# Mixture panels loaded in one 2 MB transfer each, into three double homes of the ring

## The chip, the cores and the metric

The kernel runs on one core of one Trainium2 chip. The metric is the time of one execution on the device, in microseconds (us), as the median of several runs. Five engines of the core work side by side and meet only at semaphores: TensorE (PE, with its weight loads as PEld), VectorE (DVE), ScalarE (ACT), GpSimd (POOL) and SyncE (SP). SP issues most transfers, POOL the others; all of them are carried out by the core's 16 DMA engines. "PEq" or "SPq" is the instruction queue (the sequencer) of an engine.

## The reference

Two transformer blocks in float32 over 256 tokens of width 1024. The first has a short-convolution and pooling mixer, cross attention, a dense feed-forward stage, a convolution module, cross attention again and a mixture of 8 experts. The second has a hybrid mixer (two attentions and a recurrence), attention to a memory, and a mixture of 16 experts in 4 groups. The change touches the two mixtures alone:

```python
def moe_swiglu(xn, router, w_gu, w_down):           # first: 8 experts, hidden width 3584
    ...
    for e in range(N_EXPERTS):
        out = out + comb[..., e:e + 1] * swiglu(xn, w_gu[e], w_down[e])

def swiglu(xn, w_gu, w_down):
    g, u = jnp.split(xn @ w_gu, 2, axis=-1)
    return (jax.nn.silu(g) * u) @ w_down

def _grouped_moe(x, router_w, router_b, w1, w3, w2):  # second: 16 experts, hidden width 512
    ...
    for e in range(N_EXPERTS_2):
        hid = jax.nn.silu(xt @ w1[e]) * (xt @ w3[e])
        out = out + gate_dense[:, e, None].astype(xt.dtype) * (hid @ w2[e])
```

Each token uses two experts. The weights of the first mixture are 8 x (1024 x 7168 + 3584 x 1024) floats, those of the second 16 x 3 x 1024 x 512; every one of them is read from memory once.

## The kernel before

The kernel is written directly in semaphores: for each engine there is one function (`@block.sync`, `@block.tensor`, ...) whose instructions run in the order of the text, and every meeting of two engines is a counter that one raises and the other waits for. No scheduler moves anything.

**Panels and halves.** A weight matrix comes in panels of 512 columns (gate, up) or 512 rows (down), 2 MB each. In the mixtures a panel is handled as two halves of 1 MB, [128 partitions x 2048 floats]. `stream(c)` (lines 168 to 175) lists the halves of one group of experts in the order in which they are used: gate 0, up 0, then for each further chunk gate, up, and the down panel of the chunk before, and the last down panel; each panel gives two halves that follow one another. In the first mixture a group is one expert with 7 chunks, so N = 42 halves, and 8 groups; in the second a group is 4 experts with one chunk each, so N = 24 halves, and 4 groups (`MOES`, lines 162 to 165). Together that is 8 x 42 + 4 x 24 = 432 halves.

**The ring.** `ring` (line 212) has 7 homes of one half. Half j of a group goes to home j % slots, with slots = 7 in the first mixture and 6 in the second. Outside of the mixtures the same memory is used as three homes of a whole panel (`SLOTS = 3`, `load`, lines 456 to 467), and home 6 for other things.

**The path of a half.** SP waits until the home is free and issues the transfer (lines 476 to 481). ACT waits for its landing and writes the rounded copy `w_high` (lines 1481 to 1483). DVE subtracts it from the ring's copy and writes the remainder `w_low` (lines 2055 to 2057); that raises `split`, which is both what PE waits for (line 970) and what frees the home for SP (line 479). PE then makes 12 matmuls of 512 columns with the half: four products of three matmuls each (`product`, lines 697 to 703). `w_high` and `w_low` have three places each (`SPLITS = 3`), so ACT may start on half j only when PE is done with half j - 3 (`read`, line 1482).

**What else runs in the loop.** Per chunk: ACT's silu (line 1462), DVE's gated product (line 2033), four transposes on PE (`turn_hidden`, line 965), and their split by ACT (line 1466) and DVE (line 2037). Once per group: ACT copies the last group's outputs (line 1447, before half 3), and POOL then adds them to the sums in memory with an indirect transfer of 512 KB (line 572); DVE picks the next group's tokens (line 1971, before half 8), PE finds their places (line 925), and POOL loads the rows with another indirect transfer (line 576); PE turns them before half N - 4 (line 932).

**Where the order comes from.** SP's queue holds the transfers in the order of the halves, each behind its own wait for `split`. Each home has a semaphore of its own, `landed0` and so on, raised by 16 for each transfer. The home of half j is freed by the split of half j - slots.

Of the kernel before, what the change touches and what calls it, by code (L numbers as in the profile page):

```python
# [21 lines left out]
P = 128  # L22
# [4 lines left out]
PANEL = 512  # L27
# [126 lines left out]
for _j in range(2):  # L154
# [5 lines left out]


MOES = {
    1: dict(groups=8, members=1, chunks=7, slots=7, experts=8),
    2: dict(groups=4, members=4, chunks=1, slots=6, experts=16),
}

# [32 lines left out]
def program(nc, ins, const_in, out):  # L199
    ctx = ExitStack()  # L200
    with ctx:
# [252 lines left out]
        @block.sync  # L454
        def _(sync):
            def load(i, wait):
                pieces, sem, value = panels[i]
                if wait:

                    sync.wait_ge(S(panels[i - SLOTS][1]), panels[i - SLOTS][2])  # L460
                for where, src in pieces:
                    n = src.shape[2]
                    if where == "rows":
                        dst = slot_rows(slot(i))[:, 0:src.shape[1], :]
                    else:
                        dst = slot_kn(slot(i))[:, :, where[0]:where[0] + n]
                    sync.dma_start(dst, src).then_inc(S(f"landed{slot(i)}"), 16)

            def experts(k, source):
                c = MOES[k]  # L470
                slots, halves = c["slots"], stream(c)

                sync.sem_inc(moe_sem(k, "split"), slots)

                def group(g, turn):
                    for j, (kind, chunk, half) in enumerate(halves):

                        sync.wait_ge(moe_sem(k, "split"), turn * len(halves) + (j + 1))
                        src = source(kind, g, chunk, half)
                        dst = ring[:, j % slots, :].rearrange("p (k n) -> p k n", n=src.shape[2])  # L480
                        sync.dma_start(dst, src).then_inc(moe_sem(k, f"landed{j % slots}"), 16)

                with sync.Fori(0, c["groups"]) as g:
                    group(g, g)
                sync.wait_ge(moe_sem(k, "turns_ready"), 1)
                turns = sync.value_load(count[0:1, k - 1:k], min_val=c["groups"], max_val=2 * c["groups"])
                with sync.If(turns > c["groups"]):
                    with sync.Fori(0, c["groups"]) as g:
                        group(g, g + c["groups"])
                with sync.Else():  # L490
                    sync.nop()

                if k == 1:
                    sync.wait_ge(moe_sem(k, "split"), turns * len(halves) + slots)

            last = {0: 0, 1: 10, 2: 14, 3: 36, 4: 46}
            n_dense = moe1_panel
            sync.dma_start(H[:, :, :], ins["x"][0].rearrange("(a p) d -> p a d", p=P)).then_inc(S("x_loaded"), 16)
            sync.dma_start(const[:, :], const_in[:, 0:RESIDENT]).then_inc(S("const_loaded"), 16)
            for i in range(n_dense):  # L500
                load(i, i >= SLOTS)
            for i in range(moe1_panel - SLOTS, moe1_panel):
                sync.wait_ge(S(panels[i][1]), panels[i][2])
            gu1, dn1 = ins["od_moe_gu"], ins["od_moe_down"]

            def first_mixture(kind, g, chunk, half):
                if kind == "down":
                    r = chunk * PANEL + half * 256
                    return dn1[0, bass.ds(g, 1), r:r + 256, :].rearrange("a (k p) n -> p (a k) n", p=P)
                c0 = chunk * PANEL + (7 * PANEL if kind == "up" else 0)  # L510
                return gu1[0, bass.ds(g, 1), half * 512:(half + 1) * 512, c0:c0 + PANEL]\
                    .rearrange("a (k p) n -> p (a k) n", p=P)

            experts(1, first_mixture)
            for i in range(moe1_panel, len(panels)):
                load(i, i - SLOTS >= moe1_panel)
            for i in range(len(panels) - SLOTS, len(panels)):
                sync.wait_ge(S(panels[i][1]), panels[i][2])

            second = {"gate": ins["w1_2"], "up": ins["w3_2"], "down": ins["w2_2"]}  # L520

            def second_mixture(kind, g, member, half):

                rows = 256 if kind == "down" else 512
                v = second[kind][0].rearrange("(g m) a b -> g m a b", m=4)
                return v[bass.ds(g, 1), member, half * rows:(half + 1) * rows, :].rearrange("a (k p) n -> p (a k) n", p=P)

            experts(2, second_mixture)


# [656 lines left out]
        def _(act):  # L1187
# [242 lines left out]
            def experts(k):  # L1430
# [1 line left out]
                NS, C, halves = c["slots"], c["members"] * c["chunks"], stream(c)  # L1432
                N = len(halves)
                SG = w_(2048, PANEL)
                uses = {q: sum(1 for j in range(N) if j % NS == q) for q in range(NS)}

                def gathered_high(turn):
                    act.wait_ge(moe_sem(k, "gathered"), turn + 1)
# [18 lines left out]
                with act.Fori(0, turns) as it:  # L1457
# [11 lines left out]
                    for j in range(N):  # L1469
# [8 lines left out]
                            gathered_high(it + 1)  # L1478
                            hidden_high(C - 1)

                        act.wait_ge(moe_sem(k, f"landed{j % NS}"), it * (16 * uses[j % NS]) + 16 * (j // NS + 1))
                        act.wait_ge(moe_sem(k, "read"), it * N + (j + 1))
                        A(w_high[:, j % SPLITS, :], ring[:, j % NS, :], ACT.Copy).then_inc(moe_sem(k, "high"), 1)  # L1483
                last_outputs_high()
# [842 lines left out]
```

## Time and profile before

| | |
|---|---|
| median of 3 runs | 2378.97 us (2376.46 to 2379.36) |
| profiled execution | 2376.93 us |
| its span | 2375.1 us |
| TensorE busy (matmul) | 2190.6 us, 92% |
| VectorE busy | 1694.7 us, 71% |
| ScalarE busy | 1366.7 us, 58% |
| first mixture, first to last `w_high` copy | 726.0 us to about 1680 us |
| second mixture, the same | 2063.7 us to 2341.7 us |
| bytes moved | 617.06 MB, mean 260 GB/s |

The profiled execution took 2376.93 us, of which the span covers 2375.1 us; it lies 2.04 us below the median of the three runs. The page cuts the span into 40 slices of 59.4 us. The mixtures are the slices in which TensorE, the DMA engines and the bytes per second are all high: some 15 slices for the first and nearly 5 for the second.

```
PE   7988999897978999999999999999699789599996
PEclk9999999999898999999999999999889899699998
GB/s 297 164 151 89 160 193 180 193 109 42 110 162 256 378 369 391 368 386 363 388 365 385 369 386 368 387 366 395 210 149 116 89 160 48 205 374 378 375 375 147
```

The chain of waits is the work that ended last, followed back from the end. A wait for several semaphores is put down to the one that came last. "us to landing" of a transfer runs from its issue to the raising of its semaphore.

### The profile page before, as it was taken

Reading aid. Unit: us, or ns where it says so; the run is one execution under the profiler, and the core shown is the slowest. Engines: PE = TensorE matmul, PEld = TensorE weight load, DVE = VectorE, ACT = ScalarE, POOL = GpSimd, SP = SyncE. Lnnn points to the kernel's source line nnn. Section 1 sums busy time; section 2 is a strip of 40 time slices with the busy share of each in tenths; the row PEclk is TensorE's granted clock in tenths of the full one; section 3 lists DMA queues with packets and bytes.
Section 4 is the critical chain, followed back from the end, with each engine's and each line's share of the span. In section 5 each row is a group of like instructions: output and inputs, shape, how many; then the busy total and the mean of one; then the engine's idle time right before and its main releaser. Section 6 shows DMA issues by size and latency. Waiting matters only on the chain.

```text
span 2375.1 us, 29795 instructions
## 1 busy us (share of the span) xinstructions
PE 2190.6 (92%) x11309; PEld 1847.1 (78%) x11309; DVE 1694.7 (71%) x1541; ACT 1366.7 (58%) x1195; POOL 84.7 (4%) x80
## 2 busy tenths in 40 slices
PE   7988999897978999999999999999699789599996
PEld 7867998875667888888888888888589678488884
DVE  4635454586356888888888888888746655588886
ACT  4334333405236777777777777777555343377774
POOL 2000000000000000000000000000000000100000
PEclk9999999999898999999999999999889899699998
DMA  8442455531347999999999999999643241599993
GB/s 297 164 151 89 160 193 180 193 109 42 110 162 256 378 369 391 368 386 363 388 365 385 369 386 368 387 366 395 210 149 116 89 160 48 205 374 378 375 375 147
DMA packets 274794, 617.06 MB, mean 260 GB/s; under 512 B 9520, under 2 KB 34304, under 8 KB 274720
## 3 DMA queue, kind: packets, MB, share of 16 engines
q1 hardware_dynamic: 265360, 583.39, 67.3%
q0 software_dynamic: 9360, 32.64, 4.5%
q8 instruction: 52, 0.85, 0.2%
q14 instruction: 22, 0.18, 0.0%
HBM read 603.41 MB, written 12.58 MB: 259 GB/s over the span
## 4 chain that ended last, share of the span: by engine, by line
PE 82%; DVE 4%; ACT 2%; issue 2%; ACTq 0%; POOL 0%; DVEq 0%
PE ps L701 23%; PE ps L703 23%; PE ps L702 23%; PE ps L644 2%; PE ps L965 1%; PE ps L639 1%; PE ps L863 1%; PE ps L688 1%; DVE w_low L1639 1%; PE ps L719 1%; PE ps L739 1%; PE ps L917 0%; ACT w_high L1257 0%; PE ps L932 0%; PE ps L1105 0%
## 5 line engine op out<-in xcount | busy, mean ns | idle before, releaser
L2056 DVE TENSOR_TENSOR w_low<-ring,w_high 128x2048 fp32r<-128x2048 f32 x432 | 983.1, 2290 | 146.0 <-ACT w_high L1483 145.2
L1483 ACT ACTIVATE w_high<-ring 128x2048 fp32r<-128x2048 f32 x432 | 824.2, 1917 | 156.9 <-PE ps L703 155.7
L702 PE MATMUL ps<-w_high,parts 128*128 128x512 f32 x1832 | 713.6, 390 | 0.0
L701 PE MATMUL ps<-w_high,parts 128*128 128x512 f32 x1560 | 621.9, 399 | 17.2 <-DVE w_low L2056 13.6
L703 PE MATMUL ps<-w_low,parts 128*128 128x512 f32 x1560 | 610.8, 392 | 0.0
L702 PEld LDWEIGHTS ps<-w_high,parts 128*128 128x128 f32 x1832 | 346.6, 189 | 66.8
L701 PEld LDWEIGHTS ps<-w_high,parts 128*128 128x128 f32 x1560 | 294.7, 189 | 86.6 <-issue 21.9
L703 PEld LDWEIGHTS ps<-w_low,parts 128*128 128x128 f32 x1560 | 294.3, 189 | 63.4
L1639 DVE TENSOR_TENSOR w_low<-ring,w_high 128x2048 fp32r<-128x2048 f32 (+2 forms) x109 | 243.5, 2250 | 118.5 <-ACT w_high L1257 111.6
L1257 ACT ACTIVATE w_high<-ring 128x2048 fp32r<-128x2048 f32 (+2 forms) x109 | 204.1, 1882 | 203.5 <-PE ps L703 159.4
L701 PE MATMUL ps<-XT_high,w_high 128*128 128x256 f32 x1024 | 295.9, 289 | 20.7 <-DVE parts L1628 8.9
L702 PE MATMUL ps<-XT_high,w_low 128*128 128x256 f32 x1024 | 293.5, 287 | 0.0
L703 PE MATMUL ps<-parts,w_high 128*128 128x256 f32 x1024 | 293.3, 286 | 0.0
L701 PEld LDWEIGHTS ps<-XT_high,w_high 128*128 128x128 f32 x1024 | 200.8, 196 | 23.4 <-issue 17.1
L701 PE MATMUL ps<-w_high,XT_high 128*128 128x512 f32 (+2 forms) x528 | 206.6, 391 | 0.0
L703 PE MATMUL ps<-w_low,XT_high 128*128 128x512 f32 (+2 forms) x528 | 203.0, 385 | 0.0
L702 PEld LDWEIGHTS ps<-XT_high,w_low 128*128 128x128 f32 x1024 | 200.8, 196 | 0.5
L703 PEld LDWEIGHTS ps<-parts,w_high 128*128 128x128 f32 x1024 | 200.4, 196 | 0.0
L701 PEld LDWEIGHTS ps<-w_high,XT_high 128*128 128x128 f32 x528 | 99.9, 189 | 20.2 <-DVE parts L1752 1.0
L703 PEld LDWEIGHTS ps<-w_low,XT_high 128*128 128x128 f32 x528 | 99.6, 189 | 20.1
L702 PE MATMUL ps<-w_high,XT_high 128*128 128x512 f32 x256 | 99.6, 389 | 0.0
L688 PE MATMUL ps<-const,XS 128*128 128x128 f32 x160 | 31.0, 376 | 48.8 <-DVE XS L1597 26.7
(386 smaller groups left out, 1722.3 us busy)
## 6 DMA issues: line engine op xcount, KB each, us to landing
ring<-in_od_moe_gu SPq DMA_DIRECT2D x224, 1024.0 KB, 7.9
ring<-in_od_moe_down SPq DMA_DIRECT2D x112, 1024.0 KB, 7.7
ring<-in_w SPq DMA_DIRECT2D x96, 1024.0 KB, 8.4
ring<-in_ev_ffn_gu SPq DMA_DIRECT2D x22, 1024.0 KB, 7.7
ring<-in_xa_wkv SPq DMA_DIRECT2D x8, 2048.0 KB, 8.5
ring<-in_od_pw_w SPq DMA_DIRECT2D x6, 2048.0 KB, 8.1
ring<-in_w_in SPq DMA_DIRECT2D x6, 2048.0 KB, 7.9
ring<-in_ev_ffn_down SPq DMA_DIRECT2D x11, 1024.0 KB, 5.1
```

Of the source, the lines that this page charges most:

```text
L639: last = mm(pair[:, fb // 2, fb % 2 * T:fb % 2 * T + T], w[:, kc, fb * P:(fb + 1) * P], x[:, kc, :], start=(kc == 0), stop=(kc == KC - 1))
L644: last = mm(pair[:, tc, 0:n], x[:, kc, tc * P:(tc + 1) * P], w[:, kc, 0:n], start=(kc == 0), stop=(kc == KC - 1))
L688: last = nc.tensor.transpose(ps[:, 4 + kc // 2, o:o + P], src[:, tc, kc * P:(kc + 1) * P], IDENT)
L701: mm(out_, xh, wh, start=start, stop=False)
L702: mm(out_, xl, wh, start=False, stop=False)
L703: return mm(out_, xh, wl, start=False, stop=stop)
L719: last = mm(ps[:, 4 + 2 * p + tc, h % 2 * T:h % 2 * T + T], QT[:, 2 * h + c, tc * P:(tc + 1) * P], KT[:, 2 * h + c, :], start=(c == 0), st ...
L739: last = mm(ps[:, 4 + f // 2, f % 2 * T:f % 2 * T + T], VM[:, mc, f * P:(f + 1) * P], PROBT[:, f // 2 * 2 + mc, :], start=(mc == 0), stop= ...
L1257: A(half_tile(q, w_high), half_source(q), ACT.Copy).then_inc(S("parts_high"), 1)
L1483: A(w_high[:, j % SPLITS, :], ring[:, j % NS, :], ACT.Copy).then_inc(moe_sem(k, "high"), 1)
L1639: V.tensor_tensor(half_tile(q, w_low), half_source(q), half_tile(q, w_high).bitcast(F32), SUB)\
L2056: V.tensor_tensor(w_low[:, j % SPLITS, :], ring[:, j % NS, :], w_high[:, j % SPLITS, :].bitcast(F32), SUB)\
```

## The change

The two halves of a panel come in one transfer of 2 MB. In the first mixture slots goes from 7 to 6, so both mixtures have three double homes: homes 0 and 1, 2 and 3, 4 and 5. SP skips the second half of each panel. Before it issues a panel it waits until both homes are free, which is one `split` later than the first half alone would need. One semaphore stands for a double home. ACT's wait for a half is now the wait for the whole panel; the copies themselves, still one for each half, the work on DVE and on PE, and all other waits are as before.

```diff
-    1: dict(groups=8, members=1, chunks=7, slots=7, experts=8),
+    1: dict(groups=8, members=1, chunks=7, slots=6, experts=8),
     2: dict(groups=4, members=4, chunks=1, slots=6, experts=16),
...
                 def group(g, turn):
                     for j, (kind, chunk, half) in enumerate(halves):
-
-                        sync.wait_ge(moe_sem(k, "split"), turn * len(halves) + (j + 1))
-                        src = source(kind, g, chunk, half)
-                        dst = ring[:, j % slots, :].rearrange("p (k n) -> p k n", n=src.shape[2])
-                        sync.dma_start(dst, src).then_inc(moe_sem(k, f"landed{j % slots}"), 16)
+                        if half == 1:
+                            continue
+                        sync.wait_ge(moe_sem(k, "split"), turn * len(halves) + (j + 2))
+                        src = source(kind, g, chunk)
+                        dst = ring[:, j % slots:j % slots + 2, :].rearrange("p a (k n) -> p (a k) n", n=src.shape[2])
+                        sync.dma_start(dst, src).then_inc(moe_sem(k, f"landed{j % slots // 2}"), 16)
...
-            def first_mixture(kind, g, chunk, half):
+            def first_mixture(kind, g, chunk):
                 if kind == "down":
-                    r = chunk * PANEL + half * 256
-                    return dn1[0, bass.ds(g, 1), r:r + 256, :].rearrange("a (k p) n -> p (a k) n", p=P)
+                    r = chunk * PANEL
+                    return dn1[0, bass.ds(g, 1), r:r + PANEL, :].rearrange("a (k p) n -> p (a k) n", p=P)
                 c0 = chunk * PANEL + (7 * PANEL if kind == "up" else 0)
-                return gu1[0, bass.ds(g, 1), half * 512:(half + 1) * 512, c0:c0 + PANEL]\
+                return gu1[0, bass.ds(g, 1), :, c0:c0 + PANEL]\
...
-                        act.wait_ge(moe_sem(k, f"landed{j % NS}"), it * (16 * uses[j % NS]) + 16 * (j // NS + 1))
+                        act.wait_ge(moe_sem(k, f"landed{j % NS // 2}"), it * (16 * uses) + 16 * (j // NS + 1))
                         act.wait_ge(moe_sem(k, "read"), it * N + (j + 1))
                         A(w_high[:, j % SPLITS, :], ring[:, j % NS, :], ACT.Copy).then_inc(moe_sem(k, "high"), 1)
```

On SP, in the first mixture, this is a stretch of the group around the first down panel, before. `L481 ISA` is the wait for `split`, and the numbers are partitions x blocks x floats of one transfer (4 x 512 or 2 x 1024 floats are 1 MB over 128 partitions):

```order
L481 DMA ring<-in_od_moe_gu 128x4x512
L478 REGISTER_ALU
L481 ISA
L481 DMA ring<-in_od_moe_down 128x2x1024
L478 REGISTER_ALU
L481 ISA
L481 DMA ring<-in_od_moe_down 128x2x1024
L478 REGISTER_ALU
L481 ISA
L481 DMA ring<-in_od_moe_gu 128x4x512
```

The same place after the change:

```order
L482 DMA ring<-in_od_moe_gu 128x8x512
L479 REGISTER_ALU
L482 ISA
L482 DMA ring<-in_od_moe_down 128x4x1024
L479 REGISTER_ALU
L482 ISA
L482 DMA ring<-in_od_moe_gu 128x8x512
```

Each pair of transfers and waits has become one of twice the size. On ACT, the copies of halves 5 to 8 of the first group with what each waits for, before:

```order
L1483 ACTIVATE w_high<-ring 128x2048 [waits moe1_read]
L1482 REGISTER_ALU [waits moe1_landed6]
L1483 ACTIVATE w_high<-ring 128x2048 [waits moe1_read]
L1481 REGISTER_ALU
L1482 REGISTER_ALU [waits moe1_landed0]
L1483 ACTIVATE w_high<-ring 128x2048 [waits moe1_read]
L1465 ISA
L1466 ACTIVATE parts<-ps 128x512 [waits moe1_hidden_turned]
```

and now:

```order
L1483 ACTIVATE w_high<-ring 128x2048 [waits moe1_read]
L1481 REGISTER_ALU
L1482 REGISTER_ALU [waits moe1_landed0]
L1483 ACTIVATE w_high<-ring 128x2048 [waits moe1_read]
L1482 REGISTER_ALU [waits moe1_landed0]
L1483 ACTIVATE w_high<-ring 128x2048 [waits moe1_read]
L1465 ISA
L1466 ACTIVATE parts<-ps 128x512 [waits moe1_hidden_turned]
```

Halves 6 and 7 waited for two homes (6 and 0) and now wait for one landing of double home 0. The rows of PE, DVE and POOL are the same in both programs.

## Rows read from the trace of the kernel before

**Rows 1.** The page: TensorE's busy time, and the chain's shares by engine.
```profile
PE 2190.6 (92%) x11309; PEld 1847.1 (78%) x11309; DVE 1694.7 (71%) x1541; ACT 1366.7 (58%) x1195; POOL 84.7 (4%) x80
...
PE 82%; DVE 4%; ACT 2%; issue 2%; ACTq 0%; POOL 0%; DVEq 0%
```

**Rows 2.** Busy us by stretch: PE, PEld, DVE, ACT, POOL, clock, DMA share, GB/s.
```profile
760.00:1000.00 240.00, 240.00 (x1093) 197.33 (x1093) 212.23 (x132) 183.49 (x123) 8.59 (x4) 1.00 1.02 377
...
2080.00:2300.00 220.00, 220.00 (x1005) 180.00 (x1004) 195.16 (x134) 171.58 (x118) 12.93 (x6) 1.00 1.02 375
```

**Rows 3.** Waits from 760 to 1640: us in total, times, longest us.
```profile
ACT w_high L1483 <- PE ps L703: 109.6, 178, 1.1
...
PEld ps L701 <- DVE w_low L2056: 1.8, 7, 0.3
```

**Rows 4.** SP's own waits, whole span.
```profile
SPq L481 <- DVE w_low L2056: 1017.3, 419, 44.2
```

**Rows 5.** Issues on the page: engine, operation, count, KB each, us to landing.
```profile
ring<-in_od_moe_gu SPq DMA_DIRECT2D x224, 1024.0 KB, 7.9
...
ring<-in_xa_wq SPq DMA_DIRECT2D x4, 2048.0 KB, 7.9
```

**Rows 6.** The same of the dense stage's down panels.
```profile
ring<-in_ev_ffn_down SPq DMA_DIRECT2D x11, 1024.0 KB, 5.1
```

**Rows 7.** Timeline of DVE, fourth group, halves 3 to 7: start us, us.
```profile
1096.69 2.29 DVE L2056 TENSOR_TENSOR w_low<-ring,w_high 128x2048 fp32r<-128x2048 f32 x1 [0.64 <-ACT w_high L1483]
1100.40 4.49 DVE L2056 TENSOR_TENSOR w_low<-ring,w_high 128x2048 fp32r<-128x2048 f32 x2 [1.42 <-ACT w_high L1483]
...
1105.47 4.63 DVE L2056 TENSOR_TENSOR w_low<-ring,w_high 128x2048 fp32r<-128x2048 f32 x2
```

**Rows 8.** Timeline of ACT, fourth group: halves 8 and 9, 10, 12.
```profile
1109.99 3.72 ACT L1483 ACTIVATE w_high<-ring 128x2048 fp32r<-128x2048 f32 x2
1114.49 1.92 ACT L1483 ACTIVATE w_high<-ring 128x2048 fp32r<-128x2048 f32 x1 [0.78 <-PE ps L703]
...
1120.98 1.91 ACT L1483 ACTIVATE w_high<-ring 128x2048 fp32r<-128x2048 f32 x1
```

**Rows 9.** Timeline of DVE, halves 8 and 9, then 10 and 11.
```profile
1111.94 4.49 DVE L2056 TENSOR_TENSOR w_low<-ring,w_high 128x2048 fp32r<-128x2048 f32 x2 [0.72 <-ACT w_high L1483]
...
1117.01 4.57 DVE L2056 TENSOR_TENSOR w_low<-ring,w_high 128x2048 fp32r<-128x2048 f32 x2
```

**Rows 10.** Timeline of PE, first matmul of halves 8 and 10.
```profile
1114.29 0.49 PE L701 MATMUL ps<-w_high,parts 128*128 128x512 f32 x1
...
1120.21 0.48 PE L701 MATMUL ps<-w_high,parts 128*128 128x512 f32 x1
```

**Rows 11.** Timeline of SP: the transfers of halves 10 to 13.
```profile
1099.15 9.15 SPq L481 DMA_DIRECT2D ring<-in_od_moe_gu  x4
```

**Rows 12.** Single issues, fourth group: halves 6, 8, 9 and 12, us to landing.
```profile
ring<-in_od_moe_gu SPq DMA_DIRECT2D x1, 1024.0 KB, 5.6
ring<-in_od_moe_down SPq DMA_DIRECT2D x1, 1024.0 KB, 6.7
ring<-in_od_moe_down SPq DMA_DIRECT2D x1, 1024.0 KB, 10.2
ring<-in_od_moe_gu SPq DMA_DIRECT2D x1, 1024.0 KB, 9.4
```

**Rows 13.** Timeline of POOL: the adding of rows in the fourth group.
```profile
1095.43 2.06 POOL L572 DMA_INDIRECT sums<-work,add_at  x1 [86.60 <-ACT work L1447]
```

**Rows 14.** Single issues, second mixture: halves 7 and 8 of its second group.
```profile
ring<-in_w SPq DMA_DIRECT2D x1, 1024.0 KB, 7.8
ring<-in_w SPq DMA_DIRECT2D x1, 1024.0 KB, 10.4
```

**Rows 15.** First group: DVE on halves 0 to 2, ACT on half 6.
```profile
727.97 6.70 DVE L2056 TENSOR_TENSOR w_low<-ring,w_high 128x2048 fp32r<-128x2048 f32 x3 [1.81 <-ACT w_high L1483]
...
743.97 1.93 ACT L1483 ACTIVATE w_high<-ring 128x2048 fp32r<-128x2048 f32 x1 [0.73 <-PE ps L703]
```

More of the change, by code:

```diff
@@ L520, in _, with second_mixture @@
             second = {"gate": ins["w1_2"], "up": ins["w3_2"], "down": ins["w2_2"]}
-            def second_mixture(kind, g, member, half):
-                rows = 256 if kind == "down" else 512
+            def second_mixture(kind, g, member):
                 v = second[kind][0].rearrange("(g m) a b -> g m a b", m=4)
-                return v[bass.ds(g, 1), member, half * rows:(half + 1) * rows, :].rearrange("a (k p) n -> p (a k) n", p=P)
+                return v[bass.ds(g, 1), member, :, :].rearrange("a (k p) n -> p (a k) n", p=P)
             experts(2, second_mixture)
@@ L1434, in experts @@
                 SG = w_(2048, PANEL)
-                uses = {q: sum(1 for j in range(N) if j % NS == q) for q in range(NS)}
+                uses = N // NS
                 def gathered_high(turn):
```

## The prediction, before the changed kernel was run

> **What bounds the kernel now.** I read the page first, then the table of stretches for the two mixtures, then the waits inside one of them, then SP's waits, and last the timeline of one group. The page says that TensorE has 82% of the chain and is busy for 92% of the span [rows 1]. The stretches say how tight it is where the change acts: from 760 to 1000 us TensorE is busy for 240 of 240 us at the full granted clock, and in the second mixture for 220 of 220 [rows 2]. Beside it the DMA engines are just as full, a share of 1.02 at 377 GB/s and 1.02 at 375 [rows 2]. Two things are at their limit at once, and the waits tell which leads. ACT's copies waited for PE 178 times in 880 us, 109.6 us in all; PE's weight loads waited for DVE for 1.8 us; and no row has ACT waiting for a transfer [rows 3]. SP in turn waited 1017.3 us for DVE to free a home [rows 4]. So TensorE leads, every transfer comes in time, and what transfers have is slack. The change spends that slack, so I have to measure it.
>
> **What a transfer needs.** Alone on the queue, 1 MB lands after 5.1 us [rows 6] and 2 MB after 7.9 us [rows 5]. The difference, 2.8 us for 1.05 MB, is the moving; about 2.3 us is latency that does not grow. The demand is close to the supply: in rows 2 the engines move 377 GB/s, so 1.05 MB takes 2.78 us, and TensorE goes from half 8 to half 10 in 1120.21 - 1114.29 = 5.92 us with four transposes between them [rows 10], 2.96 us for each. I take 5.5 us for moving a panel of 2 MB back to back, slightly below 2 x 2.78, since the 377 GB/s include POOL's small packets.
>
> **What the change removes.** 216 of 432 issues and waits on SP. SP waits 1017.3 us anyway [rows 4]; worth nothing. ACT gets one register instruction more or less per panel, beside its 109.6 us of waits for PE [rows 3]; worth nothing. The work on PE, DVE and POOL is the same. TensorE has no idle time in the stretches that a better supply could fill, so there is nothing on the gaining side that I can point at.
>
> **What it adds.** The time that a transfer may take, its window, becomes shorter, and the transfer longer. Before, half 10 was issued when half 3 was split: DVE ended it at 1096.69 + 2.29 = 1098.98 [rows 7], SP issued at 1099.15 [rows 11], and ACT wanted it at 1114.49 [rows 8]. That is a window of 15.3 us for landings of 7.9 us in the median [rows 5] and 10.2 at worst around there [rows 12]. Now the panel of halves 10 and 11 is issued when half 5 is split, at 1100.40 + 4.49 = 1104.89 [rows 7], plus SP's 0.17, so the window is 1114.49 - 1105.06 = 9.4 us, and the whole 2 MB must be there. The same for its neighbours: halves 8 and 9 are issued after half 3 (1099.15) and wanted at 1109.99, 10.8 us; halves 12 and 13 after half 7 (1105.47 + 4.63 = 1110.10, plus 0.17) and wanted at 1120.98, 10.7 us [rows 7, 8]. Undisturbed, 7.9 us fits into each of these with 1.5 us or more to spare, and I expect no loss there.
>
> **Where it does not fit.** Once per group POOL adds 512 KB of rows to the sums (issued at 1095.43 [rows 13]), and its packets share the 16 engines. Half 8 landed in 6.7 us and half 9, issued about 2.3 us later, in 10.2 [rows 12]. The jump is 3.5 us, of which some 0.3 us is that the issues came faster than the moving; about 3.1 us is the price of the rows. In the second mixture the jump is the same kind, 7.8 to 10.4 [rows 14]. Before, that drowned in a window of 15 us. Now the panel of halves 8 and 9 would land after 7.9 + 3.1 = 11.0 us against 10.8: late by 0.2 us. PE's own cushion behind DVE is small at this half: DVE ends half 8 at 1111.94 + 2.29 = 1114.23 and PE starts it at 1114.29 [rows 9, 10], 0.06 us. The next panel is issued 5.9 us later (1105.06 after 1099.15) and moves in 5.5, so it needs 11.0 - 0.4 = 10.6 us against 9.4, late by 1.2; there the cushion is 1120.21 - (1117.01 + 2.29) = 0.9 us [rows 9, 10], so this would lose 0.3 us, of which 0.2 have slipped already. The panel of halves 12 and 13 comes 5.2 us after it (1110.27) and needs 10.9 against 10.7, within the cushion. From there the queue drains by some 0.1 to 0.4 us per panel (panels asked for every 5.6 to 5.9 us) until POOL's second transfer of the group, which is cheaper. So with landings as quick as alone, a group loses about 0.2 to 0.3 us, one loss per group and not one per panel.
>
> **The term that decides.** Landings inside the mixtures are not as quick as alone. Half 6, before the rows are added, took 5.6 us and half 8 took 6.7, against 5.1 alone [rows 6, 12]; that is 0.5 and 1.6 us on top. Behind the first lateness each further microsecond of landing is a microsecond per group, because there is no cushion at half 8. Bounds: nothing on top (0.2 us per group; and no loss at all if the slack holds, below) and 1.6 on top (1.8 us per group). Below nothing the cost can't go, as TensorE had no idle time to give back. I take 0.4, near the row with the quickest queue, since half as many transfers should cross fewer starts; a group then loses 0.2 + 0.4 = 0.6 us. There are 8 + 4 = 12 groups: 12 x 0.6 = 7.2 us; the bounds give 2.4 and 21.6. The first group of a mixture may lose less, so I round to 6.6.
>
> **The stages' starts.** The ring is filled long before: half 6 is wanted at 743.97, and the panel of halves 6 and 7 is issued when half 1 is split, at about 732.5 [rows 15], a window of 11.3 us against 7.9. Nothing is lost, and the panels before it are loaded while TensorE is still with the router.
>
> **The sum.** 2376.93 (the profiled execution: span 2375.1 and 1.8 around it) + 6.6 = 2383.5. The median of the runs lies 2.04 us above the profiled one, so I forecast 2378.97 + 6.6 = 2385.6 us.
>
> **Rivals.** *The slack holds (not slower).* The panel of halves 8 and 9 is a down panel, whose rows are 4 KB long; if it moves faster than a gate panel and lands in 7.5 us alone, it comes at 10.6 us against 10.8, and the following panel, then late by 0.8, stays within its cushion of 0.9. It decides at landings below about 10.9 us for that panel. For it: the reckoning with 7.9 us misses the window by only 0.2 us. Against it: 6.7 us for a 1 MB half that had 5.1 alone. Time 2379, within a microsecond.
>
> *The DMA engines become the bound.* At a share of 1.02 they have hardly any idle time [rows 2], and three double homes let a transfer start only when two are free. If a panel of the loaded queue needs 9.4 us or more without POOL's help, which is 1.5 us on top of 7.9 as half 8 shows, the panels at half 10 and at the ends of the chunks are late too, and the lateness does not drain before POOL's second transfer. I price it at 1.6 to 2 us per group, 19 to 24 us: 2398 to 2403. For it: half 12 took 9.4 us even before [rows 12]. Against it: that half stood behind the rows.
>
> *Fewer, larger transfers are cheaper (faster).* The Trainium skill, "DMA: Bandwidth & Descriptors", section "Anatomy of one DMA", fits about 2.0 us fixed plus bytes over 436 GB/s per transfer, on GpSimd's path, with half the efficiency at some 860 KB; by it a panel would cost 6.8 us instead of two times 4.4. The rows agree with the form (5.1 and 7.9 give 2.3 fixed), but in the mixtures transfers overlap: at 377 GB/s a half passes every 2.78 us [rows 2, 5], so the fixed part is not paid per transfer. It would only help if ACT waited for landings, and no row has that [rows 3]. The gain that I can price is PEld's 1.8 us of waits for DVE in 880 us [rows 3], about 2.5 us over both mixtures: 2376.5; I need other relief for more. That the transfers stay at 1 MB is excluded: the sizes stand in the program.
>
> **How the numbers follow.** Forecast 0.44 (its own range 2381 to 2392), slack holds 0.34, DMA bound 0.17, faster 0.05. What a measurement can tell from no change here is 0.2%, 4.8 us. Slower by more: 0.36 of the forecast's 0.44 and the 0.17, with 0.02 of the second, 0.55. Within: 0.32 of the second, 0.08 of the forecast, 0.01 of the last: 0.41. Faster: 0.04. The range reaches from just below the second case, 2377, to 2399, where the third begins.
>
> **What the profile after would show.** Right: a new row of ACT's copies waiting for ring transfers, ten to thirty times, 10 to 30 us in all, mostly at halves 8 to 12 of a group; PE no longer busy for 240 of 240 us but for some 238.5; a landing of 8 to 9 us in the median for the 2 MB panels, 11 behind POOL's rows; the time from one group's beginning to the next up by 0.6 us. Wrong: ACT's row of waits for transfers missing or below 3 us (then the slack held), or above 60 us with waits at every chunk (then DMA bounds); PE's clock below 1.00 in these stretches; a mixture that starts later than before.

## The result, and the profile after

The change makes the kernel slower: 2399.79 us in the median of 7 runs (2391.02 to 2405.48) against 2378.76 us in 7 runs of the kernel before, a ratio of 1.0094 (95% interval 1.0076 to 1.0113; it is taken over all runs, the two medians alone give 1.0088). The forecast was 2385.6 us; its direction was right, its size a third of the measured 21 us, and the time lies just above its range. The profiled execution took 2401.29 us, its span 2399.5 us.

The page's lines that answer to [rows 1], the busy times and the chain by engine, of the kernel after:

```profile
PE 2195.2 (91%) x11309; PEld 1847.0 (77%) x11309; DVE 1693.2 (71%) x1541; ACT 1366.9 (57%) x1195; POOL 85.3 (4%) x80
...
PE 67%; DMA 8%; DVE 7%; ACT 5%; issue 4%; ACTq 0%; DVEq 0%; POOL 0%; SPq 0%
```

The work is the same, but the chain has changed hands in places: DMA, which had no share of it, has 8%, and TensorE went from 82% to 67%. The table of stretches, which answers to [rows 2] (columns: length, then busy us with counts for PE, PEld, DVE, ACT and POOL, granted clock, DMA share, GB/s), after:

```profile
760.00:1000.00 240.00, 237.89 (x1073) 195.31 (x1072) 208.65 (x128) 181.18 (x121) 8.58 (x4) 0.99 1.01 372
...
2090.00:2300.00 210.00, 204.51 (x927) 165.59 (x926) 180.02 (x122) 157.35 (x109) 10.89 (x5) 1.00 1.00 363
```

TensorE is no longer busy all the time. The DMA engines' share stays near 1, yet they move 5 and 12 GB/s less. The waits from 760 to 1640, which answer to [rows 3] (who waited for whom: us in total, times, longest us), after:

```profile
ACT w_high L1483 <- PE ps L703: 91.9, 157, 3.8
...
ACT w_high L1483 <- DMA ring<-in_od_moe_gu: 31.7, 19, 5.2
...
PEld ps L701 <- DVE w_low L2056: 11.7, 11, 2.9
PE ps L701 <- DVE w_low L2056: 9.6, 7, 2.6
```

The new row is ACT's wait for ring transfers: 19 times, up to 5.2 us. It passes through DVE to PE. The weight loads' waits for `w_low` grew from 1.8 us to 11.7; the matmuls, which had none, wait 9.6 us. These two overlap in time: TensorE's busy time in the 880 us fell from 880.0 to 870.4.

Where in a group? The fourth group again (columns of a timeline: start us, us), first SP and ACT, after:

```profile
1100.07 0.37 SPq L482 DMA_DIRECT2D ring<-in_od_moe_down  x1
1106.08 8.26 SPq L482 DMA_DIRECT2D ring<-in_od_moe_gu  x2
```

```profile
1107.36 3.71 ACT L1483 ACTIVATE w_high<-ring 128x2048 fp32r<-128x2048 f32 x2 [4.16 <-DMA ring<-in_od_moe_gu]
...
1112.42 1.93 ACT L1483 ACTIVATE w_high<-ring 128x2048 fp32r<-128x2048 f32 x1 [0.38 <-DMA ring<-in_od_moe_down]
...
1117.80 1.92 ACT L1483 ACTIVATE w_high<-ring 128x2048 fp32r<-128x2048 f32 x1 [1.18 <-DMA ring<-in_od_moe_gu]
```

These are halves 6 and 7, then 8, then 10. Then the single issues of the panels at halves 4, 6, 8 and 10 of this group, in that order, with us to landing, after ([rows 12] are those of before):

```profile
ring<-in_od_moe_gu SPq DMA_DIRECT2D x1, 2048.0 KB, 10.0
ring<-in_od_moe_gu SPq DMA_DIRECT2D x1, 2048.0 KB, 12.4
ring<-in_od_moe_down SPq DMA_DIRECT2D x1, 2048.0 KB, 12.3
ring<-in_od_moe_gu SPq DMA_DIRECT2D x1, 2048.0 KB, 11.6
```

and what PE and POOL did, after:

```profile
1111.65 0.50 PE L701 MATMUL ps<-w_high,parts 128*128 128x512 f32 x1 [1.62 <-DVE w_low L2056]
```

```profile
1096.35 2.07 POOL L572 DMA_INDIRECT sums<-work,add_at  x1 [86.55 <-ACT work L1447]
```

The panel of halves 6 and 7, issued at 1094.85, was in the air when the rows were added (1096.35 to 1106.03), and the panel of halves 8 and 9 was issued into the adding. The first took 12.4 us, ACT stood idle for 4.16 us and PE for 1.62 us. The difference is a cushion. Before, ACT started half 6 at 1102.89 and PE at 1108.74:

```profile
1102.89 1.93 ACT L1483 ACTIVATE w_high<-ring 128x2048 fp32r<-128x2048 f32 x1 [0.72 <-PE ps L703]
```

```profile
1108.74 0.48 PE L701 MATMUL ps<-w_high,parts 128*128 128x512 f32 x1
```

That is 5.85 us; after, with nothing but the work between them, it is 1111.65 - 1107.36 = 4.29. So a copy of half 6 may come 1.56 us late at no cost. The same sum gives about 1.4 us at half 10 and nothing at half 8.

Added up over each mixture, from TensorE's first product on, its idle time is 9.6 us in the first and 10.2 us in the second, where it was 0 before: 12.2 us of it at half 6, 5.5 at half 18, 1.5 at half 0 and none at half 10. Half 18 is where GpSimd's loading of the next rows is in the air (in this group issued at 1129.13, the panel at 1130.68). The longest idle stretches cost a second time. After one of 2.11 us the granted clock fell to its lower level, 1.2 GHz, for a few us, in a stretch that had the full clock before:

```profile
988.58 0.79 PE L701 MATMUL ps<-w_high,parts 128*128 128x512 f32 x1 [2.11 <-DVE w_low L2056]
```

```profile
985.00:1000.00 15.00, 12.89 (x52) 10.36 (x51) 12.65 (x11) 11.05 (x8) 0.00 (x0) 0.89 0.97 339
```

It happened again after 2.63 us (at 1354) and after 3.10 us (at 2353). The lower clock takes 7.2 us more of the two mixtures than before, which is an estimated 3.6 us of time.

Over the page the landings, which answer to [rows 5], are, after:

```profile
ring<-in_od_moe_gu SPq DMA_DIRECT2D x112, 2048.0 KB, 9.2
ring<-in_od_moe_down SPq DMA_DIRECT2D x56, 2048.0 KB, 9.1
ring<-in_w SPq DMA_DIRECT2D x48, 2048.0 KB, 10.8
```

**How the loss is split.** In each profile I take the time from the first to the last copy to `w_high` of each mixture, and the rest of the span. Before: 956.3, 276.1 and 1142.7 us. After: 970.1, 290.4 and 1139.0. So the mixtures take 28.1 us more (13.8 and 14.3) and the rest 3.7 us less. The rest is not touched by the change and moves by several us between profiles of one kernel. It mostly goes with the time that TensorE spends at the lower clock outside of the mixtures: 171 us before, 167 here, and 167 to 205 us over the 18 profiles of this case, with the longer rests at the longer times (correlation 0.91).

In the table of the experiments both parts are given against the profile before.

### The profile page after: what moved, and what is told of

The parts are those of the page before. It is cut to its first block, busy times and chain, and to the rows that moved or that the text cites. A ratio compares the mean times of both kernels' runs of the same rounds, so it can differ in the third digit from the quotient of the medians.

```text
span 2399.5 us, 28971 instructions
## 1 busy us (share of the span) xinstructions
PE 2195.2 (91%) x11309; PEld 1847.0 (77%) x11309; DVE 1693.2 (71%) x1541; ACT 1366.9 (57%) x1195; POOL 85.3 (4%) x80
## 4 chain that ended last, share of the span: by engine, by line
PE 67%; DMA 8%; DVE 7%; ACT 5%; issue 4%; ACTq 0%; DVEq 0%; POOL 0%; SPq 0%
PE ps L701 19%; PE ps L703 18%; PE ps L702 18%; DMA ring<-in_w 5%; DMA ring<-in_od_moe_gu 3%; DVE w_low L2056 3%; ACT w_high L1483 2%; PE ps L644 2%; PE ps L639 1%; PE ps L863 1%; PE ps L965 1%; PE ps L688 1%; DVE w_low L1639 1%; PE ps L719 1%; PE ps L739 1%
## 6 DMA issues: line engine op xcount, KB each, us to landing
ring<-in_w SPq DMA_DIRECT2D x48, 2048.0 KB, 10.8
```

## The experiments

Theory A, after this reading: the loss is made by the window of a whole panel (9.0 us at half 6, 9.4 to 11.5 at the others, by the trace of before), which landings under load fill and which GpSimd's two transfers of a group (adding 512 KB of rows, loading 512 KB) push over the edge. The rivals are the lost home, the late issue alone, the coarse landing alone, the size of the transfer as such, and a cost in which GpSimd has no part. A ratio is to the kernel before on the same chip; "mixtures" and "rest" are us more than in the profile before, from one profile each, and together they are what that one execution took longer. It need not be a typical one: against the median of its kernel it was 9.6 us shorter in the change without adding and in the one with a fourth double home, 6.8 shorter in the change without both, and 13.8 us longer with pairs in the first mixture only.

| kernel | ratio (95% interval) | mixtures | rest |
|---|---|---|---|
| the change | 1.0094 (1.0076 to 1.0113) | +28.1 | -3.7 |
| the change, measured again | 1.0103 (1.0073 to 1.0134) | +26.6 | +5.8 |
| six single homes | 0.9994 (0.9984 to 1.0004) | -0.1 | +1.1 |
| late issue alone | 1.0004 (0.9995 to 1.0013) | +3.9 | +4.1 |
| coarse landing alone | 1.0008 (0.9998 to 1.0017) | +1.9 | +1.4 |
| both, transfers of 1 MB | 1.0082 (1.0065 to 1.0099) | +27.3 | -5.6 |
| pairs in the first mixture only | 1.0048 (1.0027 to 1.0069) | +20.2 | +7.8 |
| fourth double home in the second | 1.0069 (1.0057 to 1.0082) | +10.1 | -2.4 |
| change without adding | 1.0055 (1.0034 to 1.0075) | +11.0 | -4.9 |
| change without loading | 1.0069 (1.0049 to 1.0090) | +9.2 | +3.8 |
| change without both | 1.0008 (0.9995 to 1.0022) | +1.7 | -3.9 |
| before without adding | 0.9999 (0.9990 to 1.0008) | +0.2 | -0.6 |

**The lost home.** Edit to the kernel before: `slots=7` becomes `slots=6` in the first mixture.

> The kernel before with six single homes in the first mixture in place of seven; everything else as before. Theory A (a panel that is in the air while GpSimd's rows are added has the narrowest window, 9.0 us at half 6; the cost comes from the pairing): the window for a single half shrinks from about 14.8 to 12 us, landings stay near 8 us (worst 10.5), no wait of ScalarE for a transfer: 0 us, at most +2. Rival C (the lost seventh home): the first mixture's share of the loss, +14 us, is here already.

No difference, and no wait for a transfer. The seventh home was not needed.

**Late issue alone.** Edit to that kernel:

```diff
-                        sync.wait_ge(moe_sem(k, "split"), turn * len(halves) + (j + 1))
+                        if half == 0:
+                            sync.wait_ge(moe_sem(k, "split"), turn * len(halves) + (j + 2))
```

> Six single homes in both mixtures, transfers of 1 MB each with their own semaphore, but both halves of a panel are issued one behind the other only when both homes are free (the late issue of the change without the large landing). Theory A: the first half then lands some 2.7 us before the second, so half 6 has its old landing of 5 to 8 us plus at most 3 of GpSimd's rows against a window of 9.0: +0 to +4 us. Rival D (the late, lumped issue lets the DMA engines run dry, and that alone costs): most of the loss, +15 to +21 us. Rival E (2 MB transfers as such move more slowly): 0 us.

+0.04%, not told from nothing. ACT does wait now and then, from 760 to 1640:

```profile
ACT w_high L1484 <- DMA ring<-in_od_moe_gu: 4.5, 5, 1.4
```

but waits of at most 1.4 us there mostly stay inside PE's cushion. In the second mixture they reach 2.8 us, and that mixture took 3.1 us more in this profile, so the late issue alone is not quite free.

**Coarse landing alone.** Edit to the kernel with six single homes:

```diff
                         act.wait_ge(moe_sem(k, f"landed{j % NS}"), it * (16 * uses[j % NS]) + 16 * (j // NS + 1))
+                        if j % 2 == 0:
+                            act.wait_ge(moe_sem(k, f"landed{j % NS + 1}"), it * (16 * uses[j % NS + 1]) + 16 * (j // NS + 1))
```

> Six single homes in both mixtures, transfers of 1 MB issued as early as before, one by one, but ScalarE waits at the first half of a panel for the landing of both (the coarse landing of the change without the late issue). Theory A: the second half is issued when the change issues the panel, but then has only 1 MB to move, so it is 1.5 to 2.7 us earlier than the whole panel: half 6 late by up to 1 us, +1 to +6 us. Rival D (late issue): 0 us. Rival F (the coarse landing alone): +15 to +21 us. If neither this nor the kernel with the late issue alone loses over 6 us, the loss needs both.

+0.08%, likewise, with the same kind of waits:

```profile
ACT w_high L1485 <- DMA ring<-in_od_moe_gu: 4.8, 4, 1.5
```

**Both, with transfers of 1 MB.** The two edits above together.

> The late issue and the coarse landing together, but with transfers of 1 MB: both halves of a panel are issued one behind the other when both homes are free, and ScalarE waits at the first half for the landing of both. Six homes. Theory A (the window of 9 to 11 us for a whole panel is the cost, whatever the transfers' size): as the change, +12 to +24 us over before. Rival G (a transfer of 2 MB is slower by itself under load): 0 to +5 us.

+0.82%, close to the change's own loss, its interval overlapping. So each half of the change is nearly free, and the two together cost 20 us. The size of the transfer has no visible part in it: from the issue of a panel's first half to the landing of both it took 9.1 us in the median of the first mixture and 10.5 in the second, where the change's transfers of 2 MB took 9.2 and 9.1, and 10.8. The split between the mixtures differs (8.7 and 18.6 us here, 13.8 and 14.3 in the change), which one profile each can't explain. The waits of the whole program show the step from harmless to costly:

```profile
PE ps L702 <- DVE w_low L2059: 30.2, 12, 6.8
ACT w_high L1486 <- DMA ring<-in_w: 30.0, 13, 5.2
ACT w_high L1486 <- DMA ring<-in_od_moe_gu: 29.8, 18, 3.5
```

ACT's longest waits are now 3.5 and 5.2 us, beyond any cushion named above. (PE's row is 13.6 us, 2 times, before: those are the starts of the two mixtures, 6.8 us each.) The Trainium skill ("DMA: Bandwidth & Descriptors", section "Bandwidth") advises to batch transfers to 1 MiB or more for three quarters of the peak rate. Halves of 1 MB meet that already, and the runs agree that 2 MB brings nothing more here: 1.0082 and 1.0094.

**The first mixture alone.** The change, with the second mixture's transfers, semaphores and waits as before.

> The change in the first mixture alone; the second mixture has six single homes as before. From the two traces the first mixture grew by 13.8 us and the second by 14.3 us, with 3.9 us given back around them. All theories: +11 to +14 us over before; if the two mixtures' losses did not add, it would be 0 or over 20.

+0.48% (+11 us), as expected, though this kernel's eight times lie far apart (2380.69 to 2404.88) and its profiled one is the longest; the second mixture took 276.1 us, as before.

**A wider window.** Edit to the change, with `home(i)` for the place of a half on ACT and DVE:

```diff
-    2: dict(groups=4, members=4, chunks=1, slots=6, experts=16),
+    2: dict(groups=4, members=4, chunks=1, slots=8, experts=16),
...
-                        dst = ring[:, j % slots:j % slots + 2, :].rearrange("p a (k n) -> p (a k) n", n=src.shape[2])
+                        two = ring[:, j % slots:j % slots + 2, :] if j % slots < 6 else w_(8192, 2, HALF)
+                        dst = two.rearrange("p a (k n) -> p (a k) n", n=src.shape[2])
```

> The change, with a fourth double home in the second mixture (in 16 KB of the work tile that is idle there); the first mixture keeps three. The window of a panel grows by two halves, 5.6 us, to 14.6 us or more. Theory A: the second mixture's +14.3 us go and the first's +11 to +14 stay: +9 to +15 us over before. Rival G (2 MB transfers slower by themselves, DMA engines short of throughput): the second mixture keeps most of its loss, +18 us or more.

In the profile the second mixture is back at 276.2 us, and PE has no idle time there,

```profile
2090.00:2300.00 210.00, 210.00 (x960) 171.91 (x959) 185.92 (x126) 163.52 (x113) 12.91 (x6) 1.00 1.03 375
```

although its panels land no sooner than in the change:

```profile
ring<-in_w SPq DMA_DIRECT2D x36, 2048.0 KB, 11.3
```

Landings of 11 us are harmless in a window of 14.6 us. So the window is the cause in the second mixture, and a shortage of DMA throughput is excluded there. The total, +0.69% (16.6 us), is a little more than the 9 to 15 expected; this kernel's first mixture took 10.0 us more in a profile that lies 9.6 us under the median. A wider window in the first mixture was not tried.

**GpSimd's transfers.** In the change and in the kernel before, the adding becomes a small plain transfer on the same semaphore:

```diff
-                    pool.indirect_dma_start(sums[k], bass.IndirectOffsetOnAxis(add_at[:, 0:1], 0), expert_out[:, :], None,
-                                            compute_op=ALU.add).then_inc(moe_sem(k, "rows_added"), 16)
+                    pool.dma_start(sums[k][T:T + 16, 0:64], expert_out[0:16, 0:64]).then_inc(moe_sem(k, "rows_added"), 16)
```

> The change, with GpSimd's indirect transfer that adds a group's rows to the sums (512 KB, 12 times) replaced by a plain one of 4 KB; the experts' outputs are therefore not added up. To be compared with the kernel before with the same replacement. Theory A as sharpened by the trace (the adding hits the panel of halves 6 and 7, whose window is the narrowest): the waits at halves 6 to 10, 46 of the 75 us that ScalarE waited for transfers, go; the loss shrinks from +21 to +4 to +10 us. Rival H (loaded landings of 9 to 11 us alone fill the window): the loss stays at +15 or more.

> The kernel before with the same replacement (the experts' outputs are not added up). TensorE is the bound there and no copy waits for a transfer, so all theories: 0 to -3 us against before; it is the base for the same replacement in the change.

Before, the adding costs nothing. In the change its removal takes 0.4 of the 0.94%: more than half is left, 13 us, which neither theory had (4 to 10, or 15 and more). So I took both away, and later the loading alone (`pool.dma_start(expert_in[0:16, 0:64], row_store[k][0:16, 0:64])` in its place):

> The change with both of GpSimd's indirect transfers of a group (adding the outputs, loading the next rows; 512 KB each) replaced by plain ones of 4 KB; neither the rows nor the sums are right then. Without the adding alone +13 us of the +21 were left, with waits at halves 16 to 22 after the loading. Theory A (landings under load of 9 us and more in windows of 9.0 to 9.7 us at halves 6, 10, 22, 28, 34, 40; GpSimd's transfers only add to it): +4 to +11 us. Rival I (GpSimd's transfers are all of it): 0 to +2 us. Rival J (they are unimportant): +13 or more.

> The change with GpSimd's adding kept and its loading of the next rows replaced by a plain transfer of 4 KB (the later groups then work on wrong rows). With both kept the loss was +21 us, without the adding +13, without both +2. If the two shares add, the adding alone gives 21 - 11 = +10 us (+6 to +14). If the adding were the whole cause, as after the first look at the trace, +18 or more; if only both together hurt, +4 or less.

Without both the loss is gone (+0.08%). That is what rival I said, and theory A, which had +4 to +11 us from landings under load alone, was wrong there: without GpSimd's transfers a loaded queue fits into the windows. The panels still land in 8.7 us (gate and up) and 8.2 us (down) in the first mixture and 9.6 in the second, in the median, yet TensorE's idle time in the two mixtures is 1.4 us in place of 19.9. What is left of the waits is harmless, since none is longer than 1.8 us:

```profile
ACT w_high L1481 <- DMA ring<-in_od_moe_gu: 15.8, 13, 1.7
...
ACT w_high L1481 <- DMA ring<-in_w: 14.9, 13, 1.8
```

With the adding alone +0.69% (15 us, just above the 6 to 14 expected), with the loading alone +0.55%, with both +0.94 and +1.03%. Each is enough for more than half of the loss in total time. Whether the shares add is open: in total time they come to a little more than the whole, within the intervals, and in the mixtures to less, 9.2 and 11.0 against 28.1 and 26.6. Where they act is plain from TensorE's idle time. With the adding alone it is 7.5 us, 6.5 of it at half 6; with the loading alone 6.9 us, 6.5 of it at half 18.

**Where in the group.** Two kernels with six homes in which some panels come whole and the others by halves, with the waits to match. First, halves 6 to 11 and 16 to 23 (those that GpSimd's transfers can meet) come one by one:

```diff
+        def alone(j):
+            return (6 <= j < 12 or 16 <= j < 24)
...
+                        if half == 1 and not alone(j):
+                            continue
+                        m = 1 if alone(j) else 2
+                        sync.wait_ge(moe_sem(k, "split"), turn * len(halves) + (j + m))
```

> Six homes; panels come in one transfer of 2 MB as in the change, except those that GpSimd's two transfers of a group can meet: halves 6 to 11 and 16 to 23 come one by one, 1 MB each, issued and waited for as before. Theory A3 (the loss is made where GpSimd's 512 KB meet a whole-panel window of 9 to 10 us, and nowhere else): -1 to +4 us against before. Rival H (every whole-panel window is too narrow under load): two thirds of the first mixture's halves are still doubled, so +8 us or more.

and the complement, `not (...)`:

> The complement: only halves 6 to 11 and 16 to 23 of a group come as whole panels of 2 MB, all others one by one as before; six homes. Theory A3: most of the change's loss, +10 to +20 us. Rival H: at most a third of it, under +8 us.

Both gave the same, 1.0044 (1.0031 to 1.0057) and 1.0043 (1.0027 to 1.0060), which together fit neither theory: the first lost more than A3 allows, the second more than rival H does. The profiles told more: the first took 2.5 us more in the mixtures and 6.6 in the rest, the second 10.7 and 0.4. So both were run again, beside the change:

> The kernel with halves 6 to 11 and 16 to 23 one by one, again, for a second profile. Theory A3: its mixtures take 0 to 4 us more than before's 956.3 + 276.1 us, and what is over lies outside of them and differs from run to run with the time at the lower clock. Rival L: the mixtures take 6 us more or longer.

> The complement again, for a second profile. The first gave 10.7 us more in the mixtures and nothing outside. Theory A3: 8 to 14 us more in the mixtures, in total +8 to +16.

> The change itself, again, on the same chip as the other three, for a second profile: 20 to 30 us more in the mixtures, +16 to +25 us in all; outside of the mixtures within 5 us of before, with either sign, going with the time at the lower clock.

1.0013 (1.0003 to 1.0024) for the first, with 1.3 us more in the mixtures, and 1.0023 (1.0012 to 1.0034) for the second, with 7.4 us more in them and 3.8 less in the rest. The second is short of what A3 had, 8 to 14 in the mixtures and 8 to 16 in all. The change itself gave 26.6 us in the mixtures, as expected, and 5.8 in the rest. The four profiles agree about the mixtures: the hit panels carry 7 to 11 us, the others 1 to 3. In total time the two are not told apart. And the two parts together make 9 to 13 us in the mixtures where the whole change makes 27 and 28: a single panel that comes by halves lets the queue recover, and a long row of whole panels does not. This last explanation is argued from the sums; it was not tested by itself.

**Longer rows, without a verdict.** In the change every panel of the mixtures was read from the down weights, `source("down", g, chunk)`, whose rows are 4 KB long (the products are then of the wrong weights).

> The change, with every panel of the mixtures, the gate and up panels too, read from the down weights, whose rows in memory are 4 KB long instead of 2 KB (the same bytes and windows; the products are of the wrong weights). In the trace of before the engines moved 409 to 418 GB/s in stretches of down panels and 385 to 389 in stretches of gate and up panels, so a panel of 2 MB moves in 5.1 instead of 5.4 us against 5.6 to 5.9 us of TensorE's demand. Theory A2 (what fills the window is the queue of an engine set that is nearly full): landings 0.5 to 1 us shorter, +2 to +10 us. Rival K (the landing under load is a fixed latency that has nothing to do with the moving rate): +15 or more.

1.0169 (1.0153 to 1.0185), slower still, with landings of 9.9 us in the first mixture's median where they had been 9.2 and 9.1. But the two mixtures went opposite ways: the first took 26.1 us more than before, the second 7.1 where the change had 14.3, with landings of 9.7 us in place of 10.8. So neither theory has a verdict. The edit also makes three panels read the same addresses, and what part that has, or the row length, is open.

## Why the prediction was right and wrong

**What bounds the kernel, and no gain.** Right. TensorE led, the DMA engines ran beside it at a busy share of 1.0, and no variant was clearly faster than before. That SP's fewer issues are worth nothing is borne out by the kernel with both halves of the change and transfers of 1 MB: it still has all 432 issues and was not slower than the change.

**The windows.** Right as worked out: 9.4 us at half 10, 10.8 at half 8. The experiments bear them out in both directions: two changes that each take away a part of the window cost no more than the runs can tell, and 5.6 us more of window undid the loss of the second mixture. The price of the adding was about right too: the prediction's 3.1 us (its own rows give 3.0, with issues 2.29 us apart against 2.78 for a move) against 3.1 in the second mixture, 9.6 to 12.7 us at half 6.

**The step that failed first: which panel meets the adding.** The prediction took the jump from half 8 to half 9 [rows 12] as the place of the rows' cost and put 3.1 us on the panel of halves 8 and 9, with its window of 10.8 us. But that panel is now issued only at about 1100, after half 9 of before had been in the air for 4 us. The panel that meets the whole adding is that of halves 6 and 7. Its window, from the split of half 1 to ACT at half 6, is the narrowest of the group, 9.0 us, and the prediction did not work it out. With the prediction's own 7.9 + 3.1 = 11.0 us it is late by 2.0 us and not by 0.2. The cushion of 1.56 us takes most of that, so this step alone moves the loss from 0.2 to about 0.4 us per group. At half 10 the prediction counted a cushion of 0.9 us. It left out the 0.6 us in which DVE makes the gated product between ACT's copy and its own work on the half, which is done by the time that a late copy comes; so the cushion is some 1.4 us, and TensorE lost nothing there, though ACT waited. In the trace the panel of half 6 landed after 12.4 us, and ACT's waits at half 6 are 17.2 of 38 us in the first mixture and 13.2 of 38 in the second.

**The term that was too small: landings under load.** This is the larger part of the miss. I added 0.4 us to 7.9; the medians are 9.2, 9.1 and 10.8 us, so 1.2 to 2.9 on top, with GpSimd's share in them. Without GpSimd's transfers they are 8.7, 8.2 and 9.6, so 0.3 to 0.8 on top in the first mixture and 1.7 in the second. I argued that half as many transfers cross fewer starts; with 1 MB transfers in the same pattern the landing of a panel was the same, so that argument had nothing in it. Once a panel at half 6 is later than its cushion, each further microsecond counts, as the prediction said of half 8: the 12.4 us of the fourth group are 3.4 late, 1.8 of it beyond the cushion. Per group the loss was 28.1 / 12 = 2.3 us in the mixtures in place of 0.6: 1.7 in the first and 3.6 in the second.

**The terms that were left out.** GpSimd's loading, which the prediction called the cheaper one and left out, is by itself enough for +0.55%, and 5.5 of TensorE's 19.9 us of idle time are at half 18. So it is not one loss per group but two. The clock that falls after long idle stretches is another term, an estimated 3.6 us.

**Luck.** The stated bound of 1.6 us on top gave 21.6 us, close to the 21 measured, but by other panels and for one loss per group; that it agrees is chance.

**The rivals.** That the slack holds fell. The case in which the DMA engines become the bound gave 2398 to 2403 us and has the measured time, with a chance of 0.17, but its mechanism is only partly right. It said that a panel needs 9.4 us or more without GpSimd's help and that the ends of the chunks are late too; without GpSimd's transfers the loss was gone, and in the change TensorE did not wait at the ends of the chunks. Engines at a share of 1.0 were not the limit where a fourth double home gave them room. It is latency against window, not throughput.

**The signs I had named.** Right: the new row of ACT's waits for ring transfers, 27 times in the first mixture, and PE at 237.9 of 240 us. Wrong: their sum, 38 us in the first mixture in place of 10 to 30 (75 in both); their place, mostly half 6 and not halves 8 to 12; the landing of 8 to 9 us, and of 11 behind the rows, which took 12.4; and 0.6 us per group. The clock below 1.00 in these stretches, which I had named as a sign of being wrong, showed too: 0.99 from 760 to 1000.

## What to carry to other kernels

When transfers are merged, the time from the last release to the first use shrinks at both ends: work out this window for every place in the loop, the narrowest first, and lay the other traffic over the new issue times and not over those of the old trace. Then add what the next engines can absorb, since an idle copy engine is not yet an idle TensorE: here it waited almost only at the halves that another queue's burst had hit. A landing time under full load is not that of a lone transfer, and a half of the slack that looks unused may be what absorbs another queue's bursts; two edits that each cost nothing may cost all of it together.

## What the runs showed of the hardware that was not expected

- The kernels at the edge scatter: the change ran from 2391.02 to 2405.48 us and the pairs in the first mixture from 2380.69 to 2404.88, while 31 runs of the kernel before, on the chip of the latter, lay within 2373.75 to 2384.77.
- One kernel measured twice, on two chips and against the kernel before each time, gave 1.0044 (1.0031 to 1.0057) and 1.0013 (1.0003 to 1.0024). The intervals do not overlap, so they understate how far two measurements may lie apart. The light stages give part of that: outside of the mixtures TensorE was at the lower clock for 205 us in the first of these profiles and 191 us in the second, against 171 in the profile before. From 1700 to 2020 us the granted clock was 0.92 before and 0.89 in the first of the two:

```profile
1700.00:2020.00 320.00, 278.38 (x1747) 253.49 (x1747) 176.48 (x215) 139.95 (x197) 4.45 (x8) 0.89 0.34 119
```

- POOL's adding of 512 KB held up a ring panel by some 3 us, though 512 KB at the 377 GB/s of [rows 2] are 1.4 us. In the second mixture the panel of halves 6 and 7 took 9.6 us in the median without GpSimd's transfers and 12.7 with the adding alone. In the first mixture of the change it took 11.9 to 13.3 us in four of the eight groups and 9.0 to 9.7 in the others; why only some are hit is open.
- TensorE's clock fell to 1.2 GHz inside a mixture after idle stretches of 2.11, 2.63 and 3.10 us, so a late transfer can cost more than the wait itself. Not every such stretch did it: in the second profile of the change one of 2.11 us (at 2322) did not.
